# Signals for the halves of a weight block, in place of signals for whole blocks

## What is computed

```python
u, z = jnp.split(x @ w_in, 2, axis=-1)             # first stack: S5 mixer, then sparse attention
kv = (h @ kv_w).reshape(bsz, seq, 6, N_KV_HEADS, HEAD_DIM)
proj = h @ w_in                                    # second stack: retention + neighbourhood attention,
q, k, v = jnp.split(proj, 3, axis=-1)              # differential attention, cross attention, and twice
def swiglu_ffn(h, w_in, w_out):                    # this, with a hidden width of 5632
    g, u = jnp.split(h @ w_in, 2, axis=-1)
    return (jax.nn.silu(g) * u) @ w_out
```

## Time and profile before

| | |
|---|---|
| median of 3 runs | 3727.26 us (3722.67 to 3729.48) |
| the profiled execution: its span | 3725.2 us, 2.1 us under the median; no other time of this execution is given |
| PE busy | 3584.0 us, 96% |
| PEld (weight loads, beside PE) | 3079.3 us, 83% |
| DVE busy | 2215.2 us, 59% |
| ACT busy | 1653.5 us, 44% |
| POOL busy | 234.2 us, 6% |
| weights loaded | 602.24 MB in the hardware queue, 55.3% of the 16 DMA engines' span |

### The profile page before, as it was taken

How to read it: one execution, slowest core, us unless ns; L and a number is a source line. 1 busy time by engine, 2 the same in 40 slices (tenths; PEclk the granted TensorE clock), 3 DMA queues, 4 the chain that set the end, 5 groups by cost and what they waited for, 6 DMA issues and landing times.

```text
span 3725.2 us, 47989 instructions
## 1 busy us (share of the span) xinstructions
PE 3584.0 (96%) x20133; PEld 3079.3 (83%) x20133; DVE 2215.2 (59%) x2908; ACT 1653.5 (44%) x2272; POOL 234.2 (6%) x236
## 2 busy tenths in 40 slices
PE   7888999999999999999999999999989999999999
PEld 6767788998987887888888888888877888888887
DVE  5997644555656655666555555555656655455554
ACT  4444434655645433454434434444433544344343
POOL 3562000000010020000000000000000000000000
PEclk9999999999999999999999999999999999999999
DMA  7334566555555664456656666566433566666664
GB/s 208 102 102 152 146 191 171 143 152 144 140 184 154 182 166 140 136 158 170 192 192 186 187 191 184 188 177 175 136 102 127 145 184 181 199 183 188 192 185 147
DMA packets 859479, 613.12 MB, mean 165 GB/s; under 512 B 10402, under 2 KB 752401, under 8 KB 858240
## 3 DMA queue, kind: packets, MB, share of 16 engines
q1 hardware_dynamic: 857168, 602.24, 55.3%
q0 software_dynamic: 2096, 7.81, 0.8%
HBM read 607.85 MB, written 2.16 MB: 164 GB/s over the span
## 4 chain that ended last, share of the span: by engine, by line
PE 83%; DVE 9%; ACT 3%; POOL 2%; issue 1%; SPq 0%; DMA 0%; DVEq 0%; ACTq 0%
PE acc L1003 27%; PE acc L992 26%; PE acc L1005 14%; PE acc L1015 10%; DVE wL L2170 3%; PE psC L1195 2%; PE psA L1164 1%; ACT wH L1522 1%; PE psA L1140 1%; DVE arena L2605 1%; PE psB L1178 1%; POOL arena L815 1%; DVE act L2143 0%; ACT arena L1494 0%; POOL mem_v L801 0%
## 5 line engine op out<-in xcount | busy, mean ns | idle before, releaser
L2170 DVE TENSOR_TENSOR wL<-ring,wH 128x1024 fp32r<-128x1024 f32 x1128 | 1346.6, 1235 | 976.5 <-ACT wH L1522 975.1
L1522 ACT CAST wH<-ring 128x1024 fp32r<-128x1024 f32 x1128 | 1126.5, 1047 | 1106.1 <-PE acc L1005 528.6
L1003 PE MATMUL acc<-act,wH 128*128 128x512 f32 x4480 | 1595.2, 400 | 8.9 <-DVE wL L2170 7.2
L1005 PE MATMUL acc<-act,wL 128*128 128x256 f32 x4480 | 1257.0, 281 | 0.0
L1003 PEld LDWEIGHTS acc<-act,wH 128*128 128x128 f32 x4480 | 843.7, 188 | 220.0 <-DVE wL L2170 9.0
L1005 PEld LDWEIGHTS acc<-act,wL 128*128 128x128 f32 x4480 | 848.3, 189 | 2.7 <-issue 1.9
L1015 PE MATMUL acc<-act,wH 128*128 128x256 f32 x2560 | 482.8, 290 | 14.7 <-DVE wL L2170 14.7
L1015 PEld LDWEIGHTS acc<-act,wH 128*128 128x128 f32 x2560 | 408.9, 195 | 19.6 <-DVE wL L2170 16.3
L992 PE MATMUL acc<-wH,act 128*128 128x512 f32 x1152 | 372.1, 399 | 8.8 <-DVE act L2162 7.7
L992 PE MATMUL acc<-wH,hidH 128*128 128x512 f32 x960 | 368.8, 393 | 6.9 <-DVE wL L2170 5.0
L1015 PE MATMUL acc<-act,wL 128*128 128x256 f32 x1280 | 366.5, 286 | 0.0
(11 more groups left out here) (357 smaller groups left out, 2734.1 us busy)
## 6 DMA issues: line engine op xcount, KB each, us to landing
ring<-in_w_ffn_in SPq DMA_DIRECT2D x176, 1024.0 KB, 5.8
ring<-in_w_ffn_out SPq DMA_DIRECT2D x88, 1024.0 KB, 5.1
ring<-in_b_w_in SPq DMA_DIRECT2D x64, 1024.0 KB, 6.3
ring<-in_w_in_ab SPq DMA_DIRECT2D x56, 1024.0 KB, 5.5
ring<-in_w_in_c SPq DMA_DIRECT2D x48, 1024.0 KB, 5.8
ring<-in_kv_w SPq DMA_DIRECT2D x24, 1024.0 KB, 5.7
ring<-in_a_w_in SPq DMA_DIRECT2D x16, 1024.0 KB, 7.4
ring<-in_w_xkv SPq DMA_DIRECT2D x16, 1024.0 KB, 5.2
```

Source lines behind the costliest of these rows:

```text
L1003: pe.matmul(bank.rearrange("p (h t) -> p h t", h=2), high[:, t, :], act2[:, t, :, :], start=t == 0, stop=False)
L1005: ins = pe.matmul(bank[:, T:2 * T], low[:, t, :], xH[:, t, :], start=False, stop=t == ph.kt - 1)
L1522: act.copy(wH[:, split_slot, cols], ring[:, slot, cols]).then_inc(h_made, 1)
L2170: dve.tensor_tensor(wL[:, split_slot, cols], ring[:, slot, cols], wH[:, split_slot, cols].bitcast(F32), ALU.subtract).then_inc(l_made, 1)
```

## The change

A second semaphore, `weight_first_halves_done`, counts on PE the last matmul that reads the first half of a block. ACT's wait in front of both casts is split in two: the first half of block n waits for the first half of block n-2 to be used (or of the block before it in the count), the second for the whole of it, as before. PE's wait in front of a block asks for the first low half alone, and a second wait, for the second low half, stands in front of the first tile of the second half. DVE's waits and SP's waits are as before.

```diff
-        blocks_done = sem("weight_blocks_done")
+        blocks_done, halves_done = sem("weight_blocks_done"), sem("weight_first_halves_done")
...
-                pe.wait_ge(l_made, ph.blocks_before(i, c, b) * 2 + 2)
+                lows = ph.blocks_before(i, c, b) * 2
+                half = ph.kt // 2
+                pe.wait_ge(l_made, lows + 1)
...
                     for t in range(ph.kt) if tiles is None else tiles:
                         k = b * ph.kt + t
+                        if t == half:
+                            pe.wait_ge(l_made, lows + 2)
...
+                        if t == half - 1:
+                            ins.then_inc(halves_done, 1)
...
                     for t in range(ph.kt):
+                        if t == half:
+                            pe.wait_ge(l_made, lows + 2)
...
+                        if t == half - 1:
+                            ins.then_inc(halves_done, 1)
...
                         for t in range(ph.kt):
+                            if f == 0 and t == half:
+                                pe.wait_ge(l_made, lows + 2)
...
+                            if f == ph.cols // P - 1 and t == half - 1:
+                                ins.then_inc(halves_done, 1)
...
+                        if j == 7:
+                            ins.then_inc(halves_done, 1)
                     ins.then_inc(blocks_done, 1)
...
                 act.wait_ge(landed[slot], landings)
-                if first >= SPLIT_SLOTS:
-                    act.wait_ge(blocks_done, number - (SPLIT_SLOTS - 1))
                 for k in halves:
+                    if first >= SPLIT_SLOTS:
+                        act.wait_ge((halves_done, blocks_done)[k], number - (SPLIT_SLOTS - 1))
                     cols = slice(k * HALF, (k + 1) * HALF)
                     act.copy(wH[:, split_slot, cols], ring[:, slot, cols]).then_inc(h_made, 1)
```

## The result

The median is 3699.72 us after the change (3696.29 to 3702.54, 4 runs), against 3726.47 us before in the runs beside it (3722.67 to 3729.48, 4 runs). The ratio is 0.9926, with a 95% interval of 0.9914 to 0.9938: 27 us faster, where 20 were forecast. The profiled execution has a span of 3698.5 us and took 3700.23 us.

The account below looks back on a forecast made before the run. PE, busy for 3584.0 of 3725.2 us, was taken as the bound; 14.7 us from stalls plus 5.1 from the clock gave 19.8, a span of 3705.4 and, with 2.1 us for the median, 3707.5 us, range 3699 to 3719.

Parts of the forecast that it names:

- part 1: PE waits for one low half instead of two before a block; stalls vanish or shrink by 1.14 us, 14.7 us together.
- the nine tok stalls: PE's waits for a low half in tok blocks, none above 0.8 us; all go, 5.3 us.
- the six short ones: PE stalls of about 0.1 us each, too short for the list of waits; counted as 0.7 us.
- The three long ones: Joined-block stalls ending at 424.82, 1158.50 and 1206.58 (1.82, 1.31, 1.86 us); they keep 0.68, 0.17 and 0.72 us.
- The first stall: First of seven L1015 stalls before 270 us, ending at 31.77; its 0.75 us goes entirely.
- Part 2: ACT casts a block's first half about 2.8 us sooner where it waits for PE; worth 0, at most 1.6 us.
- Part 3: 564 waits and 568 signals added on PE in mid-block; cost taken as 0, from above 106 us.
- Part 4: Clock drops after stalls ending at 46.00, 424.82, 1158.50, 1206.58 stay away, 1.7 us each; three of four counted, 5.1 us.
- The clock doesn't come back: Rival: stalls go, but clock drops may follow other stalls, as in attention; 3712.6 us or some more; chance 0.20.
- More comes back: Rival: all four clock drops, the two early ones and the leftovers are won, 26.5 us, 3700.8 us; chance 0.14.
- Small price: Rival: each mid-block wait costs PE 0.04 us, 22.6 us against 19.8, 3730 us, no change; chance 0.07.
- loads stopped: Rival: the mid-block wait stops weight loads running ahead, 188 ns a block, 86 us slower, 3813 us; chance 0.04.

Follow-up runs that it names:

- e3_three_pairs: Kernel before the change plus three always-met waits and three signals inside each block, some 1690 of each, nothing relaxed: 3725.49 us, ratio 1.0006.
- e2_act_only: Changed kernel, but PE again waits for both low halves ahead of a block, leaving only ACT's earlier casts: 3724.7 us, ratio 1.0004.
- e4_tok: Changed kernel with ACT's old wait and PE's start by halves in tok blocks only: 3712.1 us, ratio 0.9964.
- e5_joined: Changed kernel with ACT's old wait and PE's start by halves in joined blocks only: 3715.43 us, ratio 0.9972.
- e1_pe_only: Changed kernel with ACT's old wait ahead of both casts, leaving only PE's start by halves: 3701.01 us, ratio 0.9932.
- after_again: The changed kernel unaltered, run once more beside the other kernels: 3696.34 us, ratio 0.9930.
- e6_plain: Changed kernel with ACT's old wait and PE's start by halves only in blocks neither tok nor joined (L1015 before): 3719.58 us, ratio 0.9978.
- e7_diag_first: Changed kernel with the row diagonal made ahead of the next block's split in DVE's list: 3696.27 us, ratio 0.9921.

## Why the prediction was off by seven us

The forecast of 3707.5 us rested on the right mechanism. The step that failed is the size of part 1's terms.

**Part 1, the stalls that go: mis-sized.** The sum 5.3 + 5.6 + 0.7 = 11.6 us took each stall at its listed idle time. The steps show 18.4 us. The main cause is in every stall that goes whole: some 0.27 us that the list leaves out (0.16 under the listed end of the matmul before, 0.11 in the step behind). That is 2.4 us on top of 5.3 for the nine tok stalls, 1.0 for the four joined ones that went whole and 1.6 on top of 0.7 for the six short ones: 5.0 us. The three long ones, which were only shortened, gave 1.13, 1.14 and 1.13 us at their steps, just what the prediction took.

The other cause is six stalls with an idle time of 0.01 us or none, 1.2 us in all. The last 0.6 us are in a few other steps. Four of the six were in plain sight. The prediction took two L1015 blocks in 11.68 us as proof that the boundary between them costs nothing. In after the same two blocks take 11.50 us: the boundary held a hidden stall of 0.16 us. "No gap" in the chain is not "no stall". The conclusion drawn from these rows, that waits and signals are free, was right all the same, as e3_three_pairs shows.

**Part 1, before 330 us: right in kind.** The first stall was to go, 0.75 us. It kept 0.35 and gave 0.40, because PE came to it 0.98 us sooner than in before. That head start isn't the change's: e2_act_only, e4_tok and e5_joined, which ask for both low halves there, have 1.1 to 1.3 us of it as well. The second stall gave its 1.13 us. The work that opens the S5 stage came 3.87 us sooner (the drain at 82.53 is now at 78.66), the end of the stage 3.46 us sooner (321.55 before, 318.09 after, behind the same idle time of 7.57 us in both). The prediction had 3.05 for the stalls and 1.7 for the drop at 46.00, 4.75 together. DVE's full stretch did shift as a whole, by 4.0 us (0.98 + 0.40 + 1.13, and 1.50 from the clock). What failed is the 0.92 us of DVE's idle time ahead of the drain, which was to vanish: after has 1.01 us there. The block that is drained starts at 71.11, as soon as DVE has made its low half, and runs at a clock of 0.50 from 72.1 us on, 7.53 us for what takes 6.03 elsewhere. The drop that lay at 70.2 us in before, in an earlier block, has moved into the one that DVE waits for.

**Part 2, ACT's cast: right.** The price of 0 is what e2_act_only shows (1.0004, 0.9995 to 1.0013), and e1_pe_only has the whole gain.

**Part 3, waits and signals on PE: right.** The price is 0 by e2_act_only and at most 3 ns by e3_three_pairs. The Trainium skill ("TensorE: Matmul & The Clock Gate", section "The cost: per-tile semaphore tail") puts 26.3 ns on an increment, in a formula for the tail behind a group of small tiles in the array. The prediction carried it over to whole matmuls. By it e3_three_pairs would be an estimated 44 us slower (1690 x 26.3 ns). It is 2.2 us slower by its ratio, within the uncertainty: the rule doesn't hold for the runs of matmuls of this kernel, and the measurement decides.

**Part 4, the clock: the size about right, the reason for one drop in three.** Four drops were considered and three counted, 5.1 us. All four went (46, 425, 1159 and 1206 us), and so did the one at 94 us. The one at 70 us stayed, as a drop at 72 us, and new ones came at 20.9 and 853.8 us. A drop costs 1.5 us by the steps (1.51, 1.57 and 1.53 at 425, 1159 and 1206 us) and not 1.7; the prediction's own rows have 7.53 us against 6.04 for a block of the same stretch. After 330 us the clock gave 4.4 us, of which 1.3 are in drops at other places that are longer or shorter in one trace than in the other (after_again has 5.2 in all), and it gave 1.5 us more in the block that starts at 43.48, which were partly given back before the S5 stage. The rule used, that the drop goes with the long stall, holds at 425 us. At 1159 and 1206 us the drops also went where the stalls stayed (e4_tok, e6_plain), so there the amount was right and the reason isn't shown.

**What was not foreseen** is the stall at 1200.79 us. The prediction asked of each stall what is late next, but only among low halves. With the block before it started 1.14 us sooner, PE reached the row diagonal before DVE, which had it behind the split. It costs 1.2 us.

**The seven us in all.** Against the prediction, the stalls after 330 us gave 5.7 us more (6.8 more for the old ones, 1.2 less for the new one), the part before 330 us 0.7 less, the clock after 330 us 1.0 more and all other steps 0.95 more. The last two are luck of the profiled execution and not something that the prediction had wrong. The prediction's sign that PE's busy time would fall by some 5 us failed for the same reason as its sum: it fell by 15.1 us.

**The rivals.** "The clock doesn't come back" is out by the windows at 425, 1159 and 1206 us, though for the latter two not by its own reasons. "More comes back" has the nearest time (3700.8), but for other reasons than it gave: the two early drops and the leftovers did not all go. "Small price" and "loads stopped" are out by e3_three_pairs. The median of 3699.72 us lies at the lower edge of the range given, since neither the sum nor its upper case held anything for the unlisted part of a stall.

What stays open: e6_plain's runs give 8.2 us (4.5 to 11.9) and its trace 5.2, while the three parts' gains by their ratios sum to 0.86% and the whole is 0.68 to 0.79% (e1_pe_only and e7_diag_first). The intervals allow it, and the clock's drops differ between the three. Nothing here settles whether more is behind it.

## What to carry to other kernels

Cost a stall by the distance from one matmul's start to the next, against the same step where nothing is late, and look at the step behind it too: the idle time beside the matmul is the smaller number, and a stall of under 0.16 us has none (measured on matmuls of 512 columns). Add the hidden part only for stalls that go whole. Where a consumer reads a block's first half first, a signal for the half takes a producer's last step off every late start, and extra signals and waits in a run of full matmuls were free here. When an engine starts sooner, list everything that it takes from the engine that was late, not only the operand of the stall: the small tile behind the long one in the other's list is what it meets next.

## What was not expected of the hardware

**The step behind a stall.** The step behind a stalled matmul of 512 columns is 0.34 us in place of 0.23, at a granted clock of 1.00. It is there behind idle times of 0.11, 0.70 and 0.71 us in tok blocks and of 1.21 us in a joined block alike. Why it is longer wasn't tried.

**The clock's drops hang on more than the stall.** Stalls of 1.29 and 1.86 us in e4_tok are followed by a clock of 1.00, the same stalls in before (1.31 and 1.86 us) by 0.50. The other way round, ahead of one and the same matmul: the stall at 851.94 in after is followed by a drop (its window at 853.80 stands above), and in after_again, e1_pe_only and e7_diag_first too. The one at 862.47 in before isn't, nor are those of e2, e3, e4, e5 and e6, and all are of 1.49 or 1.50 us. In before:

```profile
862.47 0.89 PE L1195 MATMUL psC<-probT,arena 128*128 128x256 f32 x4 [1.50 <-DVE arena L2378]
```

```profile
862.90:866.30 3.40, 3.40 (x31) 3.37 (x30) 1.61 (x6) 2.11 (x6) 0.23 (x1) 1.00 0.12 36
```

In after:

```profile
851.94 0.89 PE L1209 MATMUL psC<-probT,arena 128*128 128x256 f32 x4 [1.49 <-DVE arena L2394]
```

In all of these the matmuls around the stall are the same and its time in the run differs, by up to 11.4 us. What decides wasn't tried.

**Joined blocks run at two speeds.** From one matmul to the same one 744 matmuls on, with no stall and a clock of 1.00, before takes 131.95 us and after_again 129.53. The windows that hold them, before first:

```profile
3028.12:3160.08 131.96, 131.96 (x746) 114.27 (x745) 73.48 (x76) 58.65 (x71) 0.00 (x0) 1.00 0.65 189
```

```profile
3003.08:3132.61 129.53, 129.53 (x746) 114.06 (x744) 74.23 (x75) 59.32 (x70) 0.00 (x0) 1.00 0.66 190
```

The profiled execution of after takes 131.94 us for it, e7_diag_first 129.53, e3_three_pairs 131.95 and e1_pe_only 129.52. So the two traced executions of one and the same kernel, after and after_again, differ here. In most long joined stretches of the ten traces a pair of matmuls takes 353 or 347 ns on average, and which of the two changes from stretch to stretch and from trace to trace. All steps without a stall or a low clock together gave between 4.7 us less and 4.5 us more gain than the stalls and the clock explain (e3_three_pairs and after_again), most of it by these speeds, which is about the spread of the runs. What chooses between the two wasn't found.
